# Dealing an expert's tokens over the 64 row slots in steps of four, in a one-core decoder step with a mixture of experts

## The reference

```python
eidx = grp * EXPERTS_PER_GROUP + idx               # each token: 2 of 32 experts
gate = zeros((n, N_EXPERTS)).at[arange(n)[:, None], eidx].add(wt)
hg = einsum('nd,edf->nef', xs, w_gate)             # w_gate, w_up: 32 x 2048 x 512
hu = einsum('nd,edf->nef', xs, w_up)
act = silu(hg) * hu * gate[:, :, None]
out = einsum('nef,efd->nd', act, w_down)           # w_down: 32 x 512 x 2048
```

## Time and profile before

| | us |
|---|---|
| median of 3 runs | 1805.93 (1805.49 to 1814.13) |
| the profiled execution's own time | 1807.39 |
| its span, first to last instruction | 1805.5 |
| PE busy | 1483.1 (82%) |
| PE load of weights, beside PE | 853.9 (47%) |
| DVE busy | 601.2 (33%) |
| POOL busy | 308.2 (17%) |
| ACT busy | 272.0 (15%) |
| bytes moved by DMA | 505.28 MB, mean 280 GB/s |

### The profile page before, as it was taken

How to read it: one execution, slowest core, us unless ns; L and a number is a source line. 1 busy time by engine, 2 the same in 40 slices (tenths; PEclk the granted TensorE clock), 3 DMA queues, 4 the chain that set the end, 5 groups by cost and what they waited for, 6 DMA issues and landing times.

```text
span 1805.5 us, 19311 instructions
## 1 busy us (share of the span) xinstructions
PE 1483.1 (82%) x7485; PEld 853.9 (47%) x7485; DVE 601.2 (33%) x1475; ACT 272.0 (15%) x501; POOL 308.2 (17%) x426
## 2 busy tenths in 40 slices
PE   6999898879988998798878878878877888787780
PEld 6776666567766776443333323323332333233330
DVE  2789999966654113201010100101001010010015
ACT  1100001143331001011111111111111111011111
POOL 0055555443310110000000000000000000000006
PEclk9999899999998999799889889898998989898885
DMA  9433322344513644599999999999999999999954
GB/s 268 141 96 127 105 80 95 107 137 123 171 48 79 221 187 168 215 425 427 420 410 391 408 386 403 418 397 401 396 406 394 405 401 395 397 391 399 393 211 154
DMA packets 130319, 505.28 MB, mean 280 GB/s; under 512 B 23716, under 2 KB 99700, under 8 KB 102780
## 3 DMA queue, kind: packets, MB, share of 16 engines
q1 hardware_dynamic: 112908, 493.74, 70.7%
q0 software_dynamic: 5200, 9.19, 1.6%
q10 hardware_dynamic: 12160, 1.67, 0.7%
HBM read 503.19 MB, written 26.28 MB: 293 GB/s over the span
## 4 chain that ended last, share of the span: by engine, by line
DMA 32%; PE 23%; POOL 2%; issue 1%; DVE 1%; ACT 1%; SPq 1%; POOLq 0%; ACTq 0%; DVEq 0%
DMA ring<-in_w_up_dram 31%; PE bank L1279 17%; PE bank L1300 4%; DVE arena L1820 1%; SPq L383 1%; PE bank L1246 0%; POOL arena L872 0%; POOL arena L871 0%; POOL arena L879 0%; ACT arena L720 0%; POOL arena L880 0%; ACT arena L719 0%; DMA ring<-expert_rows 0%; DVE arena L1825 0%; DMA arena<-x_rows,idx_tok 0%
## 5 line engine op out<-in xcount | busy, mean ns | idle before, releaser
L1279 PE MATMUL bank<-ring,arena 128*64 128x512 f32 x2048 | 486.0, 630 | 97.8 <-DMA ring<-in_w_up_dram 97.8
L1279 PEld LDWEIGHTS bank<-ring,arena 128*64 128x64 f32 x2048 | 196.7, 145 | 360.0 <-issue 359.9
L1300 PE MATMUL bank<-ring,arena 128*64 128x512 f32 x1024 | 277.4, 704 | 18.9 <-DVE arena L1825 18.9
L1820 DVE SCALAR_TENSOR_TENSOR arena<-arena,gcol 64x512 f32<-64x512 f32 x32 | 35.8, 1118 | 635.6 <-ACT arena L720 635.6
L948 PE MATMUL bank<-arena,ring 128*128 128x280 f32 x768 | 195.2, 415 | 0.4 <-DVE arena L1352 0.4
L848 POOL DMA_INDIRECT expert_rows<-arena,idx_dst x32 | 29.4, 920 | 952.1 <-ACT arena L725 952.1
L1300 PEld LDWEIGHTS bank<-ring,arena 128*64 128x64 f32 x1024 | 84.3, 161 | 188.6 <-issue 188.6
L948 PEld LDWEIGHTS bank<-arena,ring 128*128 128x128 f32 x768 | 150.2, 198 | 44.1 <-issue 7.6
L725 ACT ACTIVATE arena<-bank 64x512 f32<-64x512 f32 x128 | 75.7, 592 | 366.7 <-PE bank L1300 365.6
L1246 PE MATMUL bank<-ident,arena 64*128 64x64 f32 x721 | 67.9, 245 | 73.8 <-DVE arena L1820 50.3
L1209 PE MATMUL bank<-ring,arena 128*128 128x256 f32 x512 | 114.6, 386 | 0.0
(11 more groups left out here) (337 smaller groups left out, 1423.9 us busy)
## 6 DMA issues: line engine op xcount, KB each, us to landing
ring<-in_w_down_dram SPq DMA_DIRECT2D x64, 2048.0 KB, 21.2
ring<-in_w_gate_dram SPq DMA_DIRECT2D x64, 2048.0 KB, 18.2
ring<-in_w_up_dram SPq DMA_DIRECT2D x64, 2048.0 KB, 22.9
ring<-in_w_in_dram SPq DMA_DIRECT2D x20, 2048.0 KB, 8.2
ring<-in_w_out_dram SPq DMA_DIRECT2D x8, 2048.0 KB, 9.4
ring<-in_s_w_glu_dram SPq DMA_DIRECT2D x2, 2048.0 KB, 8.4
arena<-v_samples SPq DMA_DIRECT2D x8, 512.0 KB, 4.6
ring<-expert_rows SPq DMA_DIRECT2D x4, 1024.0 KB, 10.2
```

The source lines that it names most:

```text
L1279: ins = pe.matmul(PB[b][at:at + CAP, :], xgT[b][:, kk, :], slot(s, KD // 2)[:, k, :], start=(kk == 0), stop=(kk == KD - 1))
L1300: ins = pe.matmul(PB[2 + cc // 2][at:at + CAP, :], hT[:, f, :], slot(4 + half, KF // 2)[:, k, cc * 512:(cc + 1) * 512], start=(f == 0), st ...
L1820: STT(hk, sk, gcol[b][:, 0:1], uk, ALU.mult, ALU.mult).then_inc(h_made, 1)
```

## The change

`slotid` is still a constant row of the numbers 0 to 63, made once by one cast on DVE. It is now written in another order: the row is seen as 16 groups (e) of four (i), and group e, place i holds the number 16 i + e. So rank r goes to slot 4 (r mod 16) + r // 16: ranks 0 to 15 to slots 0, 4, 8, ... 60, ranks 16 to 31 to slots 1, 5, 9, ... 61, and so on. Everything that is worked out per slot follows: the gather's and the scatter's rows lie in other partitions. No instruction is added, removed or moved on any engine; the one cast reads its source with a step.

```diff
@@ -1408,7 +1408,9 @@
             nc.vector.tensor_copy(mvals[:, 0:16], iota_i[:, 0:16])
             nc.vector.tensor_copy(mvals[:, 16:33], iota_i[:, 64:81])
             nc.vector.tensor_copy(iota32, iota_i[:, 0:NE])
-            nc.vector.tensor_copy(slotid, iota_i[:, 0:CAP])
+            rows_per = CAP // 16
+            nc.vector.tensor_copy(slotid.rearrange("p (e i) -> p e i", i=rows_per),
+                                  iota_i[:, 0:CAP].rearrange("p (i e) -> p e i", i=rows_per))
             nc.vector.tensor_copy(tid, iota_i[:, 81:84])
```

## The result

| | before | changed |
|---|---|---|
| median, us | 1808.01 (5 runs) | 1798.01 (1797.24 to 1798.93, 5 runs) |
| ratio to before | | 0.9942, interval 0.9924 to 0.9961 |
| span of the profiled execution, us | 1805.5 | 1796.3 |
| PE, DVE, POOL busy, us | 1483.1, 601.2, 308.2 | 1482.9, 602.7, 306.8 |

The forecast was 1813 us. The changed kernel was timed once more later, beside other kernels on one chip: ratio 0.9954 (0.9941 to 0.9967). So the gain is 8 to 10 us by the medians. 1798 us lies inside the range given with the forecast, 1793 to 1830, but on the other side of the kernel before: the sign of the forecast was wrong.

What follows compares the result with a forecast made beforehand. The weight stream was taken to bound the kernel, 2.6 us an expert above the bare stream. Only (3) counted: +7 us on the profiled 1807.39 gave 1814.4, less 1.5 to the median, given as 1813 us; range 1793 to 1830.

Steps and rivals of the forecast that it cites:

- where a row goes: Slots of the row transfers: engine k was taken to serve slots 2k, 2k+1, 32+2k and 33+2k.
- the volleys of 8, 8 and 6: Sign in the last scatter of 22 rows: 8 begin at once, then 8, then 6, in place of 11 and 11.
- the eight engines at the end: Sign at the weight stream's end: some 8 engines left for several microseconds, in place of 2.
- (3): Rows move between DMA engines: the busiest carries 158 in place of 142, 16 more at 0.45 us, +7 us.
- (4): Congestion while a gather runs: loss in proportion to rows, which stay, so no change; ends 2.6 us more and -7 us.
- (1): The cast on DVE with a step in its source: nothing, 0.2 us if not covered.
- (2): All instructions and bytes stay, PE multiplies all 64 slots as before: nothing.
- (5): First gather no longer queues, -0.75 us; last scatter has three rows on an engine, +0.3 to +0.6 us; together nothing.
- Fewer engines gather at once: Rival: congestion during gathers eases, by 7 us or twice as much; 1799 to 1806, about 1803 us; chance 0.10.
- The four neighbours: Rival: an engine has slots 4k to 4k+3, so its busiest carries 148 fewer rows, -49 us, 1757 us; chance 0.06.
- the other upper slots: Rival: the upper 32 slots lie with other engines, so ranks 8 apart don't meet; 1789 us; chance 0.08.
- The late gather: Rival: gathered rows land later and PE waits longer for them; 1828 us; chance 0.14.

Runs made afterwards that it cites:

- e1: Against the kernel before, rank r goes to a slot of engine r mod 16, filling all sixteen engines (busiest engine 52 rows); 1786.8 us, ratio 0.9888.
- e5: Kernel before with its pairs of ranks dealt to even engines, then odd ones (busiest engine 71 rows, busiest group 101); 1799.7 us, ratio 0.9958.
- e6: The low eight: as the changed kernel, but ranks 0 to 31 on engines 0 to 7 instead of the even ones; 1810.5 us, ratio 1.0011 to before.
- e2: Against the kernel before, ranks fill the slots engine by engine, four deep (busiest engine 126 rows, busiest group 240); 1848.0 us, ratio 1.0233.

## Why the prediction was wrong

**What bounds the kernel, and where a row goes: right.** The stream and the slots that share an engine stood as read, and the volleys of 8, 8 and 6 and the eight engines at the end came as forecast.

**(3), 16 more transfers on the busiest engine for +7 us: right in kind, too high in size.** e1 and e5 have equal groups, 101 rows, and differ by 38 transfers and 0.7% (12.6 us, from two chips, each against before on its own): 0.33 us each. Removing the scatters gives 0.33 as well. By that the term is +5.3 us, within its bounds of 4.9 to 9.4; the 0.45 that I chose was too high because the excess that I put down to rows is mostly the gathers'. The run that stands nearest to the term gives less: e6 has the changed kernel's engines with its group kept as high as before (153 rows, 139 before), and all of it cost 2 us, 0 to 4 by its interval.

**(4), congestion, is the step that failed.** It said "From six gathering engines to sixteen the loss is in proportion to rows, and the rows stay, so I take no change". The rows stay, but their partitions do not. I read the loss in the windows as a price per row whatever the place. In a longer list both the rows and the filled groups are more, so those windows could not tell the two apart. The runs show that the time depends on how many gathered rows go to the same group, and the change takes the busiest group from 139 rows to 83. The shortest way through the runs goes by e6, on one chip: before to e6, more rows on the busiest engine and no relief of the group, +2.2 us; e6 to the changed kernel, the same engine loads and 70 rows less in the group, -11.0 us; together -8.8 us. As a sum of prices it comes out less closely. At 0.16 to 0.23 us, the prices of the three pairs above, 56 rows are 9 to 13 us. With +5.3 us for the engine the sum is -4 to -8 us, and measured were -10.0 and, again, -8.8 us: the sign and a part of the size, with 1 to 6 us left over. Nor do the two prices add up for e2, where they give 55 x 0.66 + 101 x 0.19 = 55 us and 42 were measured, or for e6, where they give 8 x 0.66 + 14 x 0.19 = 8 us and 2 were measured. In both the two busiest engines are neighbours, as in the kernel before; part of the one cost may hide behind the other, which no run shows.

**(1) and (2)** stood: busy times are the same. (5), under 1 us, was not measured apart.

**The rivals.** "Fewer engines gather at once", at 1799 to 1806 us, had the right sign and came within 1 us of the measured time for a wrong reason: the low eight have just as few engines and gain nothing. The four neighbours and the other upper slots are excluded by the volleys. The late gather did not come in the changed kernel. What the list of rivals lacked is the place of the rows on the tile's side of the transfer. The clue stood in the earlier trace rows: ten rows of the second volley came some 0.6 us after the first, where one row takes 0.306.

## What to carry to other kernels

The row transfers of this kernel, beside a saturated stream, had two loads to be spread, the rows on each DMA engine and the rows written into each group of partitions. Which slots belong together was read from the starts of rows in fine slices of a transfer that runs alone; what either load costs took runs that change one and keep the other. Spreading by a step in the partition index is not enough: here a step of four filled eight engines of sixteen and still gained, because it spread the groups, and the order that fills both gains twice as much, three times when it turns from one transfer to the next. Where a sum over rows explains an excess, ask which of the two directions causes it before a single price is put on all of them.

## What was not expected of the hardware

- 560 rows of 8 KB go each way, 9.19 MB together beside some 400 MB of weights; without the gathers the kernel is 62 us faster, without the scatters 24 us.
- In a scatter on free engines two neighbours that read from one group of eight partitions take 0.63 us for a row each (e6), and one alone 0.33 us (the changed kernel). In a gather on free engines neighbours took about 0.31 us each. Beside the weight stream it is the other way about: the group costs nothing that can be told in the scatters (0.7 us in 1746), but 0.16 to 0.23 us for each row of the busiest group in the gathers.
- The indirect transfers of 64 slots put slots 2k, 2k+1, 32+2k and 33+2k on one engine, by the volleys of 11 and 11 rows before, 8, 8 and 6 in the changed kernel, and 16 and 6 in e1.
